# A two-block network kernel on one NeuronCore: where the low parts of two weight units are made, how the first turned tiles take their banks, and 28 idle products between the blocks

## The reference, cut to what matters

```
# end of first_block
out = rmsnorm(mix @ w_out, g_post)            # mix: 512 x 4096
x   = x + gate[:, None] * out                 # called x1 below
# start of second_block
shift, scale, gate = split(silu(c) @ w_ada + b_ada, 3)
h    = rms_norm(x, norm_gain) * (1.0 + scale) + shift
proj = h @ w_in                               # 2048 x 8192
```

## Time and profile before

| what | value |
|---|---|
| time, median of 3 runs | 2824.46 us (2823.89 to 2824.71) |
| the profiled execution, its own time | 2822.18 us |
| its span | 2820.4 us |
| PE busy | 2772.3 us, 98% of the span |
| DVE, ACT, POOL busy | 1528.8, 1114.3 and 343.2 us |
| mean granted clock of TensorE | 0.993 of full speed |
| the chain that ended last | PE 85%, DVE 5%, ACT 2%, DMA 2% |

### The profile page before, as it was taken

The page is one execution under the profiler, slowest core; times in us unless marked ns, Lnnn a source line. Parts: engine busy times, 40 slices in busy tenths (PEclk is TensorE's granted clock), DMA queues, the critical chain, the costliest instruction groups (busy, mean ns, idle before and its releaser), DMA issues.

```text
span 2820.4 us, 33369 instructions
## 1 busy us (share of the span) xinstructions
PE 2772.3 (98%) x13174; PEld 2247.0 (80%) x13174; DVE 1528.8 (54%) x1828; ACT 1114.3 (40%) x1470; POOL 343.2 (12%) x411
## 2 busy tenths in 40 slices
PE   6999999999999999999999999899999999999999
PEld 2678888888878887888788888688878888788787
DVE  6868677765555556676752332534444434533643
ACT  7742222234344343433332332435555543432611
POOL 1011100000334223422311000200000000000000
PEclk8999999999999999999999999999999999999999
DMA  9647767754554554555455333232222223223252
GB/s 398 238 168 275 245 250 263 261 196 144 160 164 160 172 173 138 162 167 177 146 177 201 120 115 102 99 125 90 82 75 82 83 75 109 79 90 98 97 182 94
DMA packets 162122, 439.35 MB, mean 156 GB/s; under 512 B 14768, under 2 KB 59824, under 8 KB 151728
## 3 DMA queue, kind: packets, MB, share of 16 engines
q1 hardware_dynamic: 123360, 307.28, 32.5%
q0 software_dynamic: 15792, 92.99, 9.4%
q10 hardware_dynamic: 22816, 36.97, 3.7%
HBM read 398.11 MB, written 39.06 MB: 155 GB/s over the span
## 4 chain that ended last, share of the span: by engine, by line
PE 85%; DVE 5%; DMA 2%; ACT 2%; issue 1%; POOL 0%; DVEq 0%; ACTq 0%; POOLq 0%
PE PB L408 15%; PE PB L413 14%; PE PB L414 14%; PE PB L519 10%; PE PB L521 10%; PE PB L520 10%; DMA AU<-in_w_ada 1%; DVE ca L1628 1%; PE PB L636 1%; PE PB L653 1%; PE PB L411 1%; PE PB L412 1%; PE PB L416 1%; DVE AACC L1628 1%; PE PB L882 1%
## 5 line engine op out<-in xcount | busy, mean ns | idle before, releaser
L1620 DVE TENSOR_TENSOR WL<-RAW,WH 128x1024 fp32r<-128x1024 f32 (+1 forms) x422 | 513.2, 1224 | 764.7 <-ACT WH L997 581.2
L408 PE MATMUL PB<-HH,WH 128*128 128x512 f32 x2048 | 817.6, 399 | 3.5 <-ACT zp L997 1.8
L413 PE MATMUL PB<-HL,WH 128*128 128x512 f32 x2048 | 801.8, 391 | 0.0
L414 PE MATMUL PB<-HH,WL 128*128 128x512 f32 x2048 | 801.5, 391 | 0.0
L997 ACT ACTIVATE WH<-RAW 128x1024 fp32r<-128x1024 f32 (+1 forms) x424 | 433.5, 1039 | 444.6 <-PE PB L521 256.0
L519 PE MATMUL PB<-WH,HH 128*128 128x512 f32 x1248 | 490.7, 393 | 0.8 <-DVE HL L1620 0.8
L521 PE MATMUL PB<-WH,HL 128*128 128x512 f32 x1248 | 486.1, 390 | 0.0
L520 PE MATMUL PB<-WL,HH 128*128 128x512 f32 x1248 | 486.1, 390 | 0.0
L408 PEld LDWEIGHTS PB<-HH,WH 128*128 128x128 f32 x2048 | 384.9, 188 | 93.0 <-issue 9.4
L414 PEld LDWEIGHTS PB<-HH,WL 128*128 128x128 f32 x2048 | 385.3, 188 | 67.0
L413 PEld LDWEIGHTS PB<-HL,WH 128*128 128x128 f32 x2048 | 385.7, 188 | 65.8 <-issue 3.4
(11 more groups left out here) (315 smaller groups left out, 2746.0 us busy)
## 6 DMA issues: line engine op xcount, KB each, us to landing
RAW<-in_w_in_t SPq DMA_DIRECT2D x320, 512.0 KB, 3.7
AU<-in_w_ada POOLq DMA_DIRECT2D x64, 1024.0 KB, 5.5
RAW<-in_w_out_t SPq DMA_DIRECT2D x96, 512.0 KB, 3.6
bcb<-R SPq DMA_DIRECT2D x64, 256.0 KB, 6.0
S<-so ACTq DMA_DIRECT2D x24, 384.0 KB, 2.5
ebc<-R SPq DMA_DIRECT2D x32, 256.0 KB, 6.3
SY<-evb ACTq DMA_DIRECT2D x32, 256.0 KB, 2.6
yin<-SY POOLq DMA_DIRECT2D x32, 256.0 KB, 4.4
```

The costliest lines, as they stand in the source:

```text
L408: h.matmul(banks[j], lh, m.HH[:, t, :], start=st, stop=False)
L413: h.matmul(banks[j], lh, m.HL[:, t, :], start=False, stop=False)
L414: ins = h.matmul(banks[j], ll, m.HH[:, t, :], start=False, stop=en)
L1620: return h.tensor_tensor(o, a, b, op)
```

## The change

On PE, tiles 0 to 2 take their banks one at a time, each just before its first two transposes, and tile 3 is taken later and turned whole. After those transposes, 28 products of `HH`'s first 128 columns with its first tile are written to bank 0, which nobody reads before it is overwritten. On DVE, the low part of unit `AT_IN2` is made after the last `make_x1`, and `sum_x1(3)` now stands ahead of `scale_x1(2, ...)`; the low part of unit `AT_IN2 + 1` is made between the first part of `modulate2` and the loop. POOL makes neither.

```diff
--- before.py
+++ after.py
@@ -810,15 +810,18 @@
         return h.transpose(bank[:, k * 128:(k + 1) * 128], m.XR[:, k, t * 128:(t + 1) * 128], ident)
 
     def modulate2():
-        first = [take(hb, "turn2", t) for t in range(4)]
-        for t, (b, bank) in enumerate(first):
+        first = []
+        for t in range(3):
+            first.append(take(hb, "turn2", t))
             for k in range(2):
-                turn_row(t, bank, k)
-        for t, (b, bank) in enumerate(first):
-            turn_row(t, bank, 2)
+                turn_row(t, first[t][1], k)
+        for again in range(28):
+            h.matmul(PB[0] if again else reuse(0), m.HH[:, 0, 0:128], m.HH[:, 0, :], start=True, stop=True)
+        for t in range(3):
+            turn_row(t, first[t][1], 2)
         for t in range(16):
-            b, bank = first[t] if t < 4 else take(hb, "turn2", t)
-            for k in range(3 if t < 4 else 0, 4):
+            b, bank = first[t] if t < 3 else take(hb, "turn2", t)
+            for k in range(3 if t < 3 else 0, 4):
                 ins = turn_row(t, bank, k)
             ins.then_inc(*put(P.side, "turn2", t))
             drop(hb, b, ("h2", t))
@@ -2099,8 +2102,9 @@
     sum_x1(2)
     make_x1(3, 0)
     make_x1(3, 1)
+    make(AT_IN2)
+    sum_x1(3)
     scale_x1(2, 1024, 2048, 1)
-    sum_x1(3)
     scale_x1(3, 0, 512, 0)
     scale_x1(3, 512, 1024, 1)
 
@@ -2243,6 +2247,7 @@
 
     m2 = modulate2()
     next(m2)
+    make(AT_IN2 + 1)
     bg = deque([m2])
     for p in range(8):
         for k4 in range(16):
@@ -2436,22 +2441,14 @@
         G.wait_ge(*at("rx2 sum", k))
         mean_power(m.ss2[:, 20 + k:21 + k], 2048, "rx2", k)
 
-    def low(n):
-        G.wait_ge(*at("raw", n))
-        G.wait_ge(*at("hi", n))
-        G.wait_ge(*at(*slot_before(n)))
-        G.then(h.tensor_tensor(m.WL[n % 4], m.RAW[n % 3], m.WH[n % 4].bitcast(F32), ALU.subtract), "lo", n)
-
     first_factor(0)
     second_factor(0)
     first_factor(1)
     second_factor(1)
     first_factor(2)
-    low(AT_IN2)
     first_factor(3)
     second_factor(2)
     second_factor(3)
-    low(AT_IN2 + 1)
 
 
     for e in ("HL2", 15), ("XD",):
```

## The result

| | before | changed |
|---|---|---|
| median (20 executions each) | 2824.94 us | 2820.64 us |
| lowest to highest | 2820.66 to 2828.29 | 2817.24 to 2823.29 |
| span of the profiled execution | 2820.4 us | 2816.5 us |
| PE's last product of block 1 | starts 1814.36 | starts 1814.38 |
| tiles 6 to 9 turned, first transpose | 1837.59 | 1833.44 |

A forecast was written before the change was run, and what follows sets the result against it. PE, busy 2772 of 2820 us, was bound; gains lay in the passage where it waits for DVE and POOL. Savings of 3.2 to 4.2 gave 3.7 off the 2824.46 median: 2820.8 us, range 2818.7 to 2822.8.

The forecast's parts named there:

- The two holds: POOL's two low parts stretch a DVE scalar_tensor_tensor and a 512-column scaling in the passage; removing them saves 2.11 and 2.10 us.
- Giving back 0.4 at POOL's last factor: DVE's 0.75 us scaling now runs beside POOL's last factor, ending it at 1823.65 instead of 1823.25; bounds 0 and 0.9.
- The shared interface: POOL contends with DVE's two-SBUF-input subtraction; by that rule row group 2's factor ends at 1822.5, not 1821.3, saving 0.2 less.
- Costs put at nothing: Low parts on DVE, 28 products on PE and late loads are covered by waits; first low part costs 0.1 at most.
- The banks: Fourth tile's three transposes move behind row group 3's start on PE; cold, tile 5 starts after 3.1 against 2.7: 0.4 lost.
- The clock: PE's clock in the passage falls once more, late, and returns early; total saving 4.9 held, 3.5 cold like before.
- a fall just at the first products: Clock falls as PE's products start at 1827.2; may cost 1.7 us, leaving 3.2 saved.
- rival 4: Clock stays down 13.6 us over PE's products: 1 us slower, 2825.4; decides against at 8.2 us cold; chance 0.04.
- Rival 1: Clock holds through PE's turning of row group 3: 4.9 us saved, 2819.6; chance 0.22.
- Rival 2: PE's transposes do not keep or raise the clock: products start cold at 1828.0, 1.8 us saved, 2822.7; chance 0.09.
- Rival 3: The 28 idle products on PE take 0.39 us each, ending at 1826.4: 2.4 us saved, 2822.1; chance 0.05.
- Rival 5: More than 5.6 us saved, timed executions before losing up to 1.7 to the clock: 6.0 saved, 2818.5; chance 0.12.

The follow-up runs named there:

- the second part alone: Kernel before with only the second low part moved from POOL to DVE: 2823.40 against 2824.34 us, ratio 0.9998.
- the runs with one part alone: Kernel before with only the first low part on DVE (sum_x1(3) ahead of scale_x1(2)), or only the second: ratios 0.9996 and 0.9998.
- PE's program alone: Kernel before with only PE's changes (banks one by one, 28 idle products), POOL keeping both low parts: 2825.30 against 2825.41 us, ratio 1.0000.
- the low parts alone: Kernel before with both low parts on DVE and sum_x1(3) ahead of scale_x1(2), PE's program untouched: 2821.30 against 2825.41 us, ratio 0.9984.
- the second look: The changed kernel run once more, unaltered, to see its clock again: one execution, 2824.19 us, beside a median of 2824.05 before.
- the waits filled: Changed kernel with 33 idle products for 28, plus 2, 2 and 3 in later PE waits; two runs, ratios 0.9984 and 0.9985 against before.
- the scaling moved later: Changed kernel with scale_x1(2) on DVE moved behind the first tile's scale and shift: 2820.47 us; without idle products 2819.80; both ratios 0.9986 against before.

## Why the prediction was right

*The two holds.* Right in place, sign and size: 2.11 and 2.10 predicted, 3.38 - 1.28 = 2.10 measured for the first, and for the second 2.08 less on the two scalings (2.10 with the second part alone). They add up, as the runs with one part alone show. Of the 4.17 us in the profiled passage they are 3.77 (row group 3 at 9.89 in place of 13.66).

*Giving back 0.4 at POOL's last factor.* Right: 0.43 (0.62 for 0.19), and moving the scaling away gave just 0.43 back. It fell on the tensor_scalar, not on the power as I had put it. Row group 3 was turned 9.89 us after the last product, predicted 9.84.

*The shared interface.* POOL's tensor_scalar of 0.19 us took 0.62 beside a scaling and 1.13 beside a subtraction of two SBUF tensors. The Trainium skill (GPSIMD Engine Reference, Specifications) names contention with DVE instructions in a two-port mode or with two SBUF inputs. The subtraction is of the second kind; the scaling fits if it runs in a two-port mode, which no row shows. I had weighed it as 0.2 us for the low part where the change puts it; there the factor of row group 2 ended at 1821.31, predicted 1821.3 without the rule. POOL's power had started 0.98 us before the subtraction (1819.85 and 1820.83), beside the last `make_x1`, and ended 0.40 after that instruction, as the one in the prediction's row did.

*Costs put at nothing.* Right. The first low part ended before ACT's square (DVE still waited 0.15), the second used a wait (2.17 to 1.04), the products had 1.4 us of cover, the loads held up nobody: behind the passage PE has two waits above 0.12 us, of 1.09 and 0.80, and the kernel before has the same two.

*The banks, priced too high.* The sum took 0.4 us off for the fourth tile's transposes at the low clock, 11 x 0.28 = 3.1 from row group 3 to tile 5 where it was 2.7. With PE's program alone, at the low clock throughout, the products come 3.48 us behind row group 3, as before: nothing is lost. Nor do the banks one by one bring anything: in the run with the low parts alone four were taken at once and the scalings still start at 9.35.

*The clock, where the sum was mis-sized.* I gave it 3.2 to 4.2 us of total saving and called the middle the forecast. The profiled execution saved 4.17, at the edge; the second look saved 2.5 (23.23 - 20.76), outside. The step that fell short was "a fall just at the first products may cost 1.7" as the worst case, and before it the ground against rival 4, that dense products raised the clock within 1.1 us. In the low-parts run and in the second look it took 4.4 and 4.3 us of products. That is still well short of the 8.2 us at which rival 4 decides, though the 13.6 us of low clock that it reckons with did come in three variants. The fall I had put at 1826.1, 4.2 us after dense work ends; it came 3.0 us after (1824.8 and 1821.8). The 28 products did put it off, by 4.5 us against the run without them, but that bought nothing: without them the median is as good. So it is the holds that make the forecast good; that the rest fits too, 4.17 in the profile and 4.5 by the ratio for 3.7, is luck, since the clock's share is +0.4 us in one look and -1.3 in the other.

*The rivals.* Rival 1 (the clock holds) did not come in the changed kernel's two profiled executions, but did in three variants, and its size was right: with the waits filled, products start 12.87 us after the last product (predicted 12.84) and 23.23 - 18.45 = 4.8 us are saved at tiles 6 to 9 (predicted 4.9), though only 4.0 at the end of the span. Rival 2 (transposes don't raise the clock) is refuted: without the products the clock rose at 1827.3 before any product, and again with the scaling moved later (18 transposes from 1823.66, back at 1827.74, first product 1827.76). So what the Trainium skill says of transposes (TensorE: Matmul & The Clock Gate, Part 4) is not borne out here for these float32 ones. Rival 3 (0.39 us each) is refuted by 6.61 us for 28. Rival 5 can't be settled: the interval reaches 6.2 us, and the executions of one kernel spread over 6 to 8 us.

## What to carry to other kernels

When an operation on one engine takes 2 us more than its twin, look for what its neighbour was doing at that moment, here POOL beside DVE: two small helpers moved onto the engine that they disturbed paid 3.76 us for 2.4 us of work in that engine's waits. Cost such a move by the waits on both sides, and look for the next pair that it brings together. Work put into PE only to hold its clock should be tested by leaving it out: here 28 and 40 such products made no difference to the median, and 56 cost 3.4 us in the profiled passage.

## What the runs showed that I had not expected

*The clock differs between executions of one program.* Two looks at the changed kernel differ by 1.7 us in the passage with DVE's times equal to 0.02 us up to the first products; see the table. The second may be of another chip than the first, but executions of one round differ as well: the 20 executions of the changed kernel have mean granted clocks from 0.994 to 0.998. A profile's clock is one draw.

*Part of an early passage is lost again.* In the six executions whose clock is held or back before the first product, PE waits once more, before the products that follow the turning of tiles 14 and 15. Waits filled:

```profile
...
1847.65 0.47 PE L408 MATMUL PB<-HH,WH 128*128 128x512 f32 x1 [0.41 <-DVE HL L1631]
...
```

The wait is 0.18 to 0.42 us in these six, and in the other seven there is none. From tiles 6 to 9 to the end the six take 983.3 to 983.6 us, the seven 982.8 to 983.1. This is part of why holding the clock buys nothing in the end: DVE's low part of a tile is then the next to be late.

*Most of the spread comes before.* The products with the small weight block WD (L582), first seen after about 621 us, come at another time in each execution. Waits filled, then the second look at the changed kernel (first and last start at the end of the row):

```profile
...
L582 PE MATMUL PB<-HH,WD x16: 394/398/398, 620.6 to 631.2; 128*128 128x512 f32 x16
...
```

```profile
...
L582 PE MATMUL PB<-HH,WD x16: 394/398/398, 625.7 to 636.3; 128*128 128x512 f32 x16
...
```

These two are 5.1 us apart there, and 5.4 us at PE's last product of the first block (1813.23 and 1818.67). From tiles 6 to 9 to the end all thirteen executions take 982.8 to 983.6 us. What makes the first 630 us vary was not tried. The granted clock of the first 60 us doesn't order them: with a mean of 0.89 the products with WD start at 621.6, 622.3 and 624.2, with 0.80 at 621.8 to 623.9. Nor does the chip alone: two executions on the chip of the second look start them at 622.3 and 625.7.

*Who began first went through.* POOL's two low parts began 0.06 us ahead of DVE's instruction, and it was DVE that waited for their end. A POOL tensor_scalar that began beside a running DVE instruction of these kinds ended 0.04 to 0.1 us after it, a power 0.40 after it. This is read from the rows of the passage, not tested by itself.
